# Scattering finished expert blocks inside the last round of a routed mixture-of-experts kernel, and a weight ring that is 4 MB longer from the second round on

## What the reference computes

```
probs = softmax(h @ router_w + router_b)            # 256 x 8
top_p, top_i = top_k(probs, 2); top_p /= sum(top_p)
gates = one_hot(top_i) * top_p                      # 256 x 8, two non-zero in a row
out = sum over e of gates[:, e] * ((silu(h @ w_gate[e]) * (h @ w_up[e])) @ w_down[e])
x = x + g_f * out;  result = rmsnorm(x) * final_norm_g
```

## Time and profile before

| | |
|---|---|
| median of three runs | 1626.8 us (1622.92 to 1630.24) |
| profiled execution | 1625.86 us, its span 1624.0 us |
| mean granted TensorE clock | 0.968 of full speed |
| PE busy | 1475.8 us, 91% of the span |
| HBM traffic | 478.10 MB read, 303 GB/s over the span |
| loads of expert weights | 168 of 2048 KB |
| blocks in a round, rounds | 22, 7 |

### The profile page before, as it was taken

How to read it: one execution, slowest core, us unless ns; L and a number is a source line. 1 busy time by engine, 2 the same in 40 slices (tenths; PEclk the granted TensorE clock), 3 DMA queues, 4 the chain that set the end, 5 groups by cost and what they waited for, 6 DMA issues and landing times.

```text
span 1624.0 us, 43674 instructions
## 1 busy us (share of the span) xinstructions
PE 1475.8 (91%) x19378; PEld 1108.4 (68%) x19378; DVE 367.6 (23%) x1004; ACT 160.3 (10%) x374; POOL 141.5 (9%) x230
## 2 busy tenths in 40 slices
PE   4998999999998897799999889989989889989996
PEld 2886878888886786666667567557657557656665
DVE  1724230120202703211144311111111111111112
ACT  2103110111111212100000000000000000000000
POOL 0000041240300000000100000000000000000000
PEclk9999999999999998999999999999999999999998
DMA  9847486647519417249979989997997997997950
GB/s 386 364 146 267 190 325 238 259 182 272 195 53 379 166 52 311 105 186 387 419 331 418 425 375 369 427 425 314 428 426 317 427 425 321 415 425 330 415 243 27
DMA packets 43767, 493.86 MB, mean 304 GB/s; under 512 B 4848, under 2 KB 5104, under 8 KB 5232
## 3 DMA queue, kind: packets, MB, share of 16 engines
q1 hardware_dynamic: 41040, 475.02, 71.6%
q10 hardware_dynamic: 2592, 16.73, 2.5%
HBM read 478.10 MB, written 13.63 MB: 303 GB/s over the span
## 4 chain that ended last, share of the span: by engine, by line
PE 77%; DMA 16%; DVE 4%; issue 1%; ACT 1%; POOLq 0%; POOL 0%; ACTq 0%; SPq 0%; DVEq 0%
PE PS L692 27%; PE PS L398 19%; DMA ring<-in_expert_stream 15%; PE PS L701 13%; PE PS L557 5%; PE PS L376 3%; PE PS L749 2%; PE PS L366 1%; DVE arena L983 1%; PE PS L383 1%; PE PS L672 1%; DMA arena<-in_positions 1%; PE PS L606 1%; PE PS L524 1%; PE PS L536 1%
## 5 line engine op out<-in xcount | busy, mean ns | idle before, releaser
L692 PE MATMUL PS<-ring,arena 128*32 128x256 f32 x9856 | 580.2, 385 | 71.0 <-DMA ring<-in_expert_stream 59.4
L692 PEld LDWEIGHTS PS<-ring,arena 128*32 128x32 f32 x9856 | 369.8, 111 | 248.8 <-DMA ring<-in_expert_stream 50.2
L983 DVE TENSOR_TENSOR arena<-arena,PS 128x128 f32<-128x128 f32 (+2 forms) x299 | 108.9, 364 | 979.4 <-ACT arena L942 549.0
L398 PE MATMUL PS<-arena,ring 128*128 128x256 f32 x1408 | 316.2, 385 | 3.5 <-ACT arena L912 1.7
L701 PE MATMUL PS<-ring,arena 128*32 128x256 f32 x4928 | 303.7, 385 | 0.9 <-DVE arena L1356 0.9
L398 PEld LDWEIGHTS PS<-arena,ring 128*128 128x128 f32 x1408 | 270.3, 193 | 45.9 <-issue 6.8
L701 PEld LDWEIGHTS PS<-ring,arena 128*32 128x32 f32 x4928 | 187.3, 112 | 89.8 <-issue 10.7
L1479 POOL COPY arena<-arena 128x256 f32 x153 | 61.5, 402 | 842.3 <-PE PS L692 793.7
L942 ACT ACTIVATE arena<-PS 128x128 f32<-128x128 f32 x154 | 43.1, 280 | 832.0 <-PE PS L692 832.0
L764 ACT ACTIVATE arena<-PS 128x512 f32<-128x512 f32 (+3 forms) x104 | 59.9, 589 | 284.9 <-PE PS L398 69.5
L557 PE MATMUL PS<-arena,ring 128*128 128x256 f32 x352 | 80.1, 387 | 0.0
(11 more groups left out here) (177 smaller groups left out, 567.0 us busy)
## 6 DMA issues: line engine op xcount, KB each, us to landing
ring<-in_expert_stream SPq DMA_DIRECT2D x168, 2048.0 KB, 18.0
ring<-in_dense_stream SPq DMA_DIRECT2D x105, 1024.0 KB, 6.9
ssm_scratch<-arena ACTq DMA_DIRECT2D x12, 1024.0 KB, 4.3
ring<-ssm_scratch SPq DMA_DIRECT2D x12, 1024.0 KB, 16.9
arena<-in_xt ACTq DMA_DIRECT2D x1, 1024.0 KB, 13.8
arena<-in_ssm_small ACTq DMA_DIRECT2D x1, 1024.0 KB, 21.5
out_t<-arena ACTq DMA_DIRECT2D x1, 1024.0 KB, 3.9
consts<-in_consts ACTq DMA_DIRECT2D x1, 670.5 KB, 9.3
```

Of the source, the lines that this page charges most:

```text
L398: mm = pe.matmul(PS[:, bank, j * T:(j + 1) * T], w[:, c, j * P:(j + 1) * P], moving[:, c, :], start=(c == 0), stop=(c == NC - 1))
L692: mm = pe.matmul(PS[32 * q:32 * q + 32, 0, 0:256], hbuf[:, c * BLK:(c + 1) * BLK], w[:, q * 256:(q + 1) * 256], start=(c == 0), stop=(c == ...
L983: return dve.tensor_tensor(o_, a, b, op)
```

## The change

1. `scatter` is a helper that PE calls in the last round. It multiplies one finished block, held in `accb` (256 columns), by its gate rows, held in `gtb` (256 columns), into banks 4 to 7. It is called once with both zeroed before the round's first gate_up, then after each e_down of the loop, and twice behind the last e_down. Only blocks that exist are scattered.
2. In the last round DVE waits for the scatter of the block before, writes the finished sum into `accb` instead of `acc` (`keep_last`), and makes the three gate-row operations for that block there. In round 1 it no longer makes them.
3. `gts` is gone. POOL's two memsets of 3072 columns are gone too, with the waits for them; two of 256 columns take their place.
4. The freed columns hold `more`, two slots of 2 MB. Loads 24 and 25 (the first two of round 1) go there, and from load 26 on the ring has 9 places: load n goes where load n-9 was. Load 24 waits, on SP, for the last gather and for `spread_psum`, since `more` lies over the gather's operands.
5. Small buffers move into `stat` and into constants that are no longer read.

```diff
+def pair_plan():
+    plan, last, queue = [], {}, list(range(RING // 2))
+    for n in range(PAIRS):
+        if n < RING // 2:
+            s = n
+        elif MORE_AT <= n < MORE_AT + MORE:      # MORE, MORE_AT = 2, EXPERTS * STEP (= 24)
+            s = RING // 2 + n - MORE_AT
+            queue.append(s)
+        else:
+            s = queue.pop(0)
+            queue.append(s)
+        plan.append((s, last.get(s)))
+        last[s] = n
+    return plan
...
@@ SyncE
-            for i in range(RING, ROUNDS * EXPERTS * STEP, 2):
-                step, k = divmod(i - RING, STEP)
-                rnd, e = divmod(step, EXPERTS)
-                if k == 0:
-                    sp.wait_ge(gu_done, upto[e] + upto[-1] * rnd)
-                if k == GU:
-                    sp.wait_ge(down_done, upto[e] + upto[-1] * rnd)
-                load_pair(i)
+            for n in range(RING // 2, PAIRS):
+                prior = PAIR_PLAN[n][1]
+                if prior is None:
+                    sp.wait_ge(e_gather, GATHERS)
+                    sp.wait_ge(spread_psum, 1)
+                else:
+                    step, k = divmod(prior, STEP)
+                    rnd, e = divmod(step, EXPERTS)
+                    sp.wait_ge(gu_done if k < GU else down_done, upto[e] + upto[-1] * rnd)
+                load_pair(n)
...
@@ TensorE
+            def scatter(first=False, last=False):
+                for h in range(2):
+                    for q in range(4):
+                        rows = slice(BLK * q, BLK * q + BLK)
+                        mm = pe.matmul(PS[:, 4 + q, h * T:(h + 1) * T], accb[rows, h * P:(h + 1) * P], gtb[rows, :],
+                                       start=(first and h == 0), stop=last, skip_group_check=True)
+                mm.then_inc(e_scat, 1)
...
+                if rnd == ROUNDS - 1:
+                    pe.wait_ge(part_zeroed, 1)
+                    pe.wait_ge(reps_ready, 1)
+                    scatter(first=True)
...
                        pe.wait_ge(hidT_ready, first)
                        pe.wait_ge(acc_done, first)
                        e_down(at - STEP)
+                        if e and rnd == ROUNDS - 1:
+                            pe.wait_ge(gt_ready, upto[e - 1])
+                            scatter()
...
                        e_down(at)
+                        if rnd == ROUNDS - 1:
+                            pe.wait_ge(gt_ready, j)
+                            scatter()
...
             e_down(expert_at(ROUNDS - 1, EXPERTS - 1))
 
-            pe.wait_ge(gt_ready, upto[-1] * 1)
-            pe.wait_ge(gts_zeroed, 1)
-            pe.wait_ge(acc_zeroed, 1)
+            pe.wait_ge(gt_ready, upto[-1])
+            scatter()
+            pe.wait_ge(gt_ready, upto[-1] + 1)
             pe.wait_ge(acc_done, upto[-1] * ROUNDS + 1)
-            for j in range(MOST):
...
+            scatter(last=True)
...
@@ VectorE
                     dve.wait_ge(down_done, j + blocks * rnd)
-                    keep(wide_block(acc, j - 1), rnd).then_inc(acc_done, 1)
+                    if rnd < ROUNDS - 1:
+                        keep(wide_block(acc, j - 1), rnd).then_inc(acc_done, 1)
                     dve.wait_ge(e_hid, j + blocks * rnd + 1)
                     turn_hid().then_inc(hidT_ready, 1)
-                    if rnd == 1:
+                    if rnd == ROUNDS - 1:
+                        dve.wait_ge(e_scat, j + 1)
+                        keep_last(j - 1)
                         dve.wait_ge(gt_ready, j)
-                        gate_rows(j)
+                        gate_rows(j - 1)
             dve.wait_ge(down_done, blocks * ROUNDS)
-            keep(wide_block(acc, blocks - 1), ROUNDS - 1).then_inc(acc_done, 1)
+            dve.wait_ge(e_scat, blocks + 1)
+            keep_last(blocks - 1)
+            dve.wait_ge(gt_ready, blocks)
+            gate_rows(blocks - 1)
+            dve.wait_ge(e_scat, blocks + 2)
...
@@ GpSimd
-            pool.memset(acc[:, LEAST * EXPERTS * 256:], 0.0).then_inc(acc_zeroed, 1)
...
-            pool.memset(gts[:, LEAST * EXPERTS * 256:], 0.0).then_inc(gts_zeroed, 1)
+            pool.memset(accb, 0.0)
+            pool.memset(gtb, 0.0).then_inc(part_zeroed, 1)
```

More of the change, by code:

```diff
@@ L57 @@
 W_IN, W_OUT, SSM, GLU = 12, 4, 3 * BATCHES, 8
+MORE, MORE_AT = 2, EXPERTS * STEP
 MOD_GROUPS = 24
@@ L154, in trunk_kernel @@
         work = arena[:, 4096:14336]
-        extra = arena[:, 14336:16768]
-        acc = arena[:, 16768:16768 + MOST * 256]
+        more = arena[:, MOST * 256:MOST * 256 + MORE * 2 * PIECE]
+        extra = arena[:, MOST * 256 + MORE * 2 * PIECE:MOST * 256 + MORE * 2 * PIECE + 1612]
+        acc = arena[:, MOST * 256 + MORE * 2 * PIECE + 1612:]
         ssm_par, bb, pows, phasor = acc[:, 0:2048], acc[:, 2048:3072], acc[:, 3072:4096], acc[:, 4096:6144]
@@ L225, in trunk_kernel @@
         hg = arena[:, 0:MOST * 256]
-        gts = arena[:, MOST * 256:2 * MOST * 256]
-        h_tm, sel, places, spread = gts[:, 0:2048], gts[:, 2048:3840], gts[:, 3840:4736], gts[:, 4736:5760]
+        h_tm, sel, places, spread = more[:, 0:2048], more[:, 2048:3840], more[:, 3840:4736], more[:, 4736:5760]
         o = 0
@@ L233, in take @@
             o += n
-            assert o <= 2432
+            assert o <= 1612
             return extra[:, o - n:o]
-        hbuf, e_act_b, e_hid_b, hidT = take(256), take(SLOT), take(SLOT), take(SLOT)
-        reps, gtmp = take(1024), take(256)
+        hbuf, hidT, reps = take(256), take(SLOT), take(1024)
+        e_act_b, e_hid_b = stat[:, 0:SLOT], stat[:, SLOT:2 * SLOT]
+        gtmp, accb, gtb = consts[:, 0:256], consts[:, 496:752], consts[:, 752:1008]
         r = [take(16) for _ in range(7)]
@@ L292, in expert_at, with pair_slot, pair_sem, pair_full @@
             return (rnd * EXPERTS + e) * STEP
-        def pair_full(i):
-            at = i % RING
-            return ring_full[at], 16 * (sum(n % RING == at for n in range(PRE)) + i // RING + 1)
+        def pair_slot(n):
+            s = PAIR_PLAN[n][0]
+            if s < RING // 2:
+                return ring[:, 2 * s * PIECE:(2 * s + 2) * PIECE]
+            s -= RING // 2
+            return more[:, 2 * s * PIECE:(2 * s + 2) * PIECE]
+        def pair_sem(n):
+            s = PAIR_PLAN[n][0]
+            return ring_full[2 * s] if s < RING // 2 else (more_full0, more_full1)[s - RING // 2]
+        def pair_full(n):
+            s = PAIR_PLAN[n][0]
+            dense_uses = sum(m % RING == 2 * s for m in range(PRE)) if s < RING // 2 else 0
+            return pair_sem(n), 16 * (dense_uses + sum(PAIR_PLAN[m][0] == s for m in range(n + 1)))
         def blocks_upto(eng):
@@ L322, in _, with load_pair @@
                 load(DENSE + SSM + n, dense_in[DENSE + n])
[L324 to L329, removed]
-                load_pair(i)
+            def load_pair(n):
+                sp.dma_start(pair_slot(n), expert_in[n]).then_inc(pair_sem(n), 16)
+            for n in range(RING // 2):
+                sp.wait_ge(piece_done, 1 + max(m for m in range(PRE) if m % RING in (2 * n, 2 * n + 1)))
+                load_pair(n)
             sp.wait_ge(items_ready, 1)
             upto = blocks_upto(sp)
-            for i in range(RING, ROUNDS * EXPERTS * STEP, 2):
-                step, k = divmod(i - RING, STEP)
-                rnd, e = divmod(step, EXPERTS)
-                if k == 0:
-                    sp.wait_ge(gu_done, upto[e] + upto[-1] * rnd)
-                if k == GU:
-                    sp.wait_ge(down_done, upto[e] + upto[-1] * rnd)
-                load_pair(i)
+            for n in range(RING // 2, PAIRS):
[7 more added lines that the diff above has]
+                    sp.wait_ge(gu_done if k < GU else down_done, upto[e] + upto[-1] * rnd)
+                load_pair(n)
         AT_BT, AT_T, AT_CT = DENSE, DENSE + BATCHES, DENSE + 2 * BATCHES
@@ L1365, in gate_rows, with keep_last @@
                 sid = col(consts, j + C_SID)
-                dve.scalar_tensor_tensor(wide_block(gts, j), reps[:, 0:256], sid, reps[:, 512:768], ALU.is_equal, ALU.mult)
+                dve.scalar_tensor_tensor(gtb, reps[:, 0:256], sid, reps[:, 512:768], ALU.is_equal, ALU.mult)
                 dve.scalar_tensor_tensor(gtmp, reps[:, 256:512], sid, reps[:, 768:1024], ALU.is_equal, ALU.mult).then_inc(gate_part, 1)
                 dve.wait_ge(gate_part, j + 1)
-                tt(wide_block(gts, j), wide_block(gts, j), gtmp, ALU.add).then_inc(gt_ready, 1)
+                tt(gtb, gtb, gtmp, ALU.add).then_inc(gt_ready, 1)
+            def keep_last(j):
+                tt(accb, wide_block(acc, j), PS[:, 1, 0:256], ALU.add).then_inc(acc_done, 1)
             dve.wait_ge(items_ready, 1)
             blocks = dve.value_load(items[0:1, EXPERTS - 1:EXPERTS], min_val=LEAST * EXPERTS, max_val=MOST)
-            dve.wait_ge(acc_zeroed, 1)
             for rnd in range(ROUNDS):
@@ L1385, in _ @@
                 turn_hid().then_inc(hidT_ready, 1)
-                if rnd == 1:
+                if rnd == ROUNDS - 1:
```

(10 more changed lines are left out.)

19 lines of the change are left out of this document (10 added, 9 removed).

## The result

The changed kernel takes 1573.16 us (median of four runs, 1570.35 to 1591.74) against 1628.52 us for the kernel before in the same comparison. The ratio is 0.968, with a 95% interval of 0.9634 to 0.9726. The forecast was 1573. The profiled execution took 1573.05 us, its span 1571.2 us, 52.8 us less than before.

The account below looks back on a forecast made before the run. The prediction held that neither PE nor DMA bounds alone: the ring is too short to carry DMA over the long expert. Terms -38.0 - 5.2 + 10.5 - 21.1 = -53.8 led to 1573 us, range 1558 to 1588.

Parts of the forecast that it names:

- rounds 2 to 5: Four expert rounds: from 129.3 to 119.8 us each, with loads at 420 GB/s, -38.0 us.
- round 6: Last round: PE-bound by 22 blocks with a scatter call each, 140.7 us against 130.2, +10.5 us.
- tail to the residual: After the last round: 28.0 us shrink to 6.9 us as most scatters move into the round, -21.1 us.
- The mechanism: Expert rounds: two more ring places, 9.98 us of loading, close DMA's 8 us hole; DMA's rate then bounds.
- The signs that the prediction named: Rounds 2 to 6: no long-expert slice below 350 GB/s, load waits 25 to 35 us, period 6.3 us, tail under 8.
- The load-by-load working: Ring model for the expert rounds, fitted to seven places (129.0 us a round); nine places give 119.8 us.
- The scatter call: Each call in round 6: 0.875 us of matmuls plus 0.27 for two form changes, 1.15 us.
- that are gone anyway: Round 6: of the 25.3 us of scatter, some 15 lie in waits that vanish anyway.
- the ring brings nothing: Rival on the ring: loads slow down in the queue or the places don't enter the rotation; 1616 us, chance 0.04.
- Ring not quite continuous: Rival on the ring: each round still loses 2.5 us at the hole, four rounds 10; 1583 us, chance 0.10.
- Form changes at 1 us: Rival on round 6's scatter calls: form changes cost 1 us instead of 0.27; 1590 us, chance 0.08.
- Serial last round: Rival on round 6: PE stands still during DVE's part between scatter and next block; 1632 us, chance 0.03.

Follow-up runs that it names:

- e8: Changed kernel with every load from number 26 on cut to 3584 of its 4096 columns: 1548.08 us.
- e2: Changed kernel with one extra place in the ring (load 24) instead of two: 1599.80 us.
- e3: Changed kernel with three extra places in the ring (loads 24 to 26), the third taken from the accumulator's columns: 1574.39 us.
- e6: Changed kernel with the scatter's 8 matmuls in the loop written as 128 x 32 weights, so PE never changes form there: 1572.37 us.
- e1: Changed kernel with no extra places, so the ring stays at seven and the scatter stays inside round 6: 1624.22 us, ratio 0.9972 to the kernel before.
- e4: Changed kernel with nine places kept but the scatter put back behind the last round, all blocks using one block's gate rows: 1573.75 us.
- e5: Changed kernel without the matmuls of the 22 scatters behind real blocks, the waits between PE and DVE kept: 1555.8 us.

## Why the prediction was right

Against the trace, term by term:

| term | forecast | measured |
|---|---|---|
| before round 0 | 0 | -4.6 |
| round 0 | 0 | -0.1 |
| round 1 | -5.2 | -5.8 |
| rounds 2 to 5 | -38.0 | -34.2 |
| round 6 | +10.5 | +11.6 |
| tail to the residual | -21.1 | -21.0 |
| behind the residual | 0 | +1.3 |
| sum | -53.8 | -52.8 |

The measured terms are differences of row times: round 6 from 1400.65 to 1536.01 + 6.39 = 1542.40, or 141.8 us against 130.2; the tail from there to 1549.41, 7.0 us against 28.0.

**The mechanism** stood. The hole at the long expert closed with two places (DMA view), the bound moved to DMA's rate (e8), one place would have been too few and three are no better (e2, e3). The signs that the prediction named came true: no slice below 350 GB/s at the long expert beside an SP wait of 24.0 us, load waits of 25.5 us, a period of 6.39 us, a tail of 7.0 us. The load-by-load working was fitted to seven places, so seven confirm nothing; it was 4 us of stage off for nine places, and the steps from nine to eight and from nine to ten came within 1 and 4 us of it.

**Rounds 2 to 5** were sized 119.8 us and took 120.7, 3.8 us more in four. The assumed rate is not what was off: DMA moved 420 GB/s over these 482.9 us, as taken. Two small things add up. Loads landed 5.01 us apart on average (97 loads, 914.30 to 1400.46 us), where the sum had 4.99; that is 2 us. And the 97 are one load more than 4 x 24: at the first gate_up of round 6 DMA is further ahead of what the round needs than it was at that of round 2. 50.3 MB in 120.7 us would be 417 GB/s, but more than 50.3 MB was loaded.

Half of the loads of this stage land at most 4.89 us behind the one before. What the average has above that is 2.9 us a round. 1.1 us of it stand at two loads of each round, those that SP issues 3.7 to 5.1 us before the landing ahead of theirs, behind its long wait and shortly after; the other 1.8 us stand at loads issued earlier, and nothing here says why. The two slices of 363 GB/s in round 3 (1098.6 to 1104.6 us) lie behind SP's long wait too, where only two or three loads are issued and not landed.

Of the 15.3 us a round over PE's own 114.0 in the kernel before, the prediction gave 8.5 to waits, from a mean over seven rounds. In rounds 2 to 5 it is 10.7 us idle and 4.6 us of slower matmuls. This split does not enter its sum. The two ends of its range hold slips below 1 us (426 GB/s make 118.1 us a round, not 117.9; 1.2 us in five rounds are 6, not 5).

**The scatter call** was sized 1.15 us, measured 1.21: 0.86 of matmuls and 0.35 for the two changes of form, where I took 0.27. The rule of the Trainium skill that spoke against the change ("TensorEngine Tiling (Array Packing)", Key Properties: a change of tiling mode drains the engine) agrees with e6 against the changed kernel, and the price here is some 7 us a run (22 x 0.35 = 7.7, and 7.0 by the stage).

**The start** was not forecast: 4.6 us came from code that the change hardly touches, and e1 to e8, with the same code there, spread over 12 us. Without it and the end the profiled execution had gained 49.5 us, not 53.8. The stage fell 4.3 us short of the sum, and a start 4.6 us earlier, of which the sum knew nothing, made up for it: that the median fell on the forecast to 0.2 us is chance in that part.

**The split was misleading.** The forecast booked +10.5 - 21.1 = -10.6 us to the scatter. Round 6 and tail take 158.2 us before, 151.8 with the scatter's move alone (e1), 148.3 with the places alone (e4) and 148.8 with both. So the two gains do not add up, since both use the same waits of round 6. In e1 the round takes 144.4 us (1457.79 to 1595.78 + 6.39), 14.2 more than before, though the 22 calls are 26.6 us of PE: 12 of them lie where PE waited or ran slowly before. In e4, with no scatter in the round, the places take 10.0 us out of it (115.0 us up to the last block's start, 1406.83 to 1521.81, where before it took 125.0, 1445.31 to 1570.30). The 15 us of waits "that are gone anyway" could be used by either; once the places have them, the scatter's move brings nothing (0.5 us the other way). The rival "the ring brings nothing" put its case at 1616 us with "about +10 in round 6"; e1 measured 1624, with +14.2.

**The rivals.** Ring not quite continuous: so in small, with 1.1 us a round at the loads issued late, where the rival had 2.5, and no slice of round 3 below 363 GB/s. Form changes at 1 us: 0.35. Serial last round: e5's period is 5.18 us with all the waits in place, as DVE's part (1505.08 to 1506.74 us for one block of e5) ends before the gate_up beside it does (1504.57 to 1508.03).

## What to carry to other kernels

When two engines are both nearly full, look at the DMA rate in fine slices over one period of the schedule: a slice at 0 beside waits of PE in the same period points at a buffer that is too short for the longest consumer. Here the width of the hole over the time of one load (9 us over 5) was the number of places missing, and one place halved it. A hole without such waits costs nothing, as e8 shows. Memory that is freed can be worth the whole gain, while the work that was moved to free it is worth nothing beside it: two changes that fill the same waits must not be booked separately. Once the hole is closed, shorten what bounds next (here bytes in rounds 1 to 5, PE in the last), and leave the places alone.

## What was not expected of the hardware

In rounds 2 to 5 of the changed kernel PE still waits for loads, up to 3.0 us at a time, and the granted clock is 1.00 by its rounded mean, its level of 2.4 GHz; before, with 33 such waits in seven rounds instead of 16, it was 0.97 over the same rounds and 0.94 in one 29 us stretch. Some of what the ring gave back came as clock: 13 of the 34 us are PE's busy time. The length of a wait does not tell by itself whether the clock falls: in the changed kernel it fell to 0.50, the level of 1.2 GHz, beside the wait of 2.48 us that ends at 1054.56, and it did not behind those of 3.01 us (to 926.09) and 2.72 us (to 1295.2). Why was not tried.

DMA holds 420 GB/s for 483 us on end. The Trainium skill, "DMA: Bandwidth & Descriptors", Bandwidth, names about 358 GB/s as what binds a core for HBM to SBUF, and 425 as measured with the pair's other core idle. This kernel runs on one core, and the trace agrees with the second.
